# Expert stage of a decoder layer: another order of ScalarE and GpSimd work per block, and a down projection in three products of halves

## The chip, the core and the metric

The kernel runs on one core of a Trainium2 chip. The metric is device time in microseconds (us) of one execution. The core has a matrix engine (TensorE; PE in the rows, PEld its weight loads), VectorE (DVE), ScalarE (ACT), GpSimd (POOL), SyncE (SP), which here only issues transfers, and 16 DMA engines that all queues share. Each engine takes its own instructions in the order in which they are written. Engines wait for one another by semaphores.

## What is computed

One layer, depth 1, with 2048 tokens of width 1024: a gated linear recurrence with its projections, and then a mixture of 16 experts, two per token, and a last norm. The change lies in the expert stage:

```python
g = jnp.einsum('bsd,edf->bsef', h, w_gate)      # w_gate, w_up: 16 x 1024 x 256
u = jnp.einsum('bsd,edf->bsef', h, w_up)
act = jax.nn.silu(g) * u * gates[..., None]     # gates: two nonzero per token
out = jnp.einsum('bsef,efd->bsd', act, w_down)  # w_down: 16 x 256 x 1024
x = x + g2[:, None, :] * out
return rmsnorm(x, final_norm_g)
```

## The kernel before

Three stages follow one another: norm and recurrence (lines below 670), the output projection with routing (`out_and_route`), and the experts (`experts`, lines 1220 to 1668). Routing sorts the pairs of token and expert into **blocks** of 128 rows; each block belongs to one expert, and the 16 experts have 39 blocks together in this execution. The residual rows lie in DRAM as `x_slots` (`dr["x2"]`), by slot; the rows that the experts read lie in `hn_slots`.

A block `b` goes through these steps, each written as a small function:

- **TensorE** (`expert_tensor`): `turn` transposes the rows `e_xg` into PSUM (L1587). `gate_up` multiplies them with the gate and up weights, as three products of halves: high by high, high by low, low by high, 24 matmuls (L1610 to L1612). `turn_act` transposes the activation (L1618). `down` multiplies it with the down weights in fp32 (L1631), four matmuls of 512 columns, two records each in the trace. The loop runs `gate_up(i+2)` with `turn_act(i+1)` inside it, `turn(i+3)`, `down(i+1)`.
- **ScalarE** (`expert_scalar`): `tanh`, `high_x` (the high half of the rows, with `load_h`, which issues the load of the next `e_xg`), `high_a` (copies the turned activation to `e_ah`), `load_x` (issues the load of the residual rows `e_xa`), `square` (sum of squares of the new residual rows, L1454), `scale_row` (rows times the inverse root, to `e_obs`), `high_w` (high halves of the weights of an expert to come, in two parts of two quarters, each where it is due), and `index_acc` and `index_out` (the row numbers of the two scatters, L1432 and L1438).
- **VectorE** (`expert_vector`): `act_product`, `low_x`, `y_scaled` and `accumulate` (`e_ab` = down output plus `e_xa`, L1546), `low_w` (low halves of weights).
- **GpSimd** (`expert_gpsimd`): `scatter_acc` writes `e_ab` back to `x_slots` (L1316); `root` makes the inverse root in four small steps (L1340 to L1348); `weigh` multiplies `e_obs` with the norm's gain into `e_ob` (L1332); `scatter_out` scatters `e_ob` to the output (L1323).
- **SyncE** (`expert_sync`): 48 small loads of records (L1265), and the loads of the weights of 16 experts in four quarters each (`load_quarter`, L698 to L703). A quarter's buffer is loaded again once it is converted.

The order of the work is written out by hand. What matters below is which buffers exist once: `e_idx_o`, the row numbers of `scatter_out`, and `e_ob`, its rows. `index_out(b)` waits until `scatter_out(b-1)` has landed (`out_done`), `weigh(b)` too. `root(b)` waits for `square(b)`, `scale_row(b)` for `root(b)` and for `weigh(b-1)`, `square(b)` for `accumulate(b)`.

Of the kernel before, what the change touches and what calls it, by code (L numbers as in the profile page):

```python
# [4 lines left out]
F32 = mybir.dt.float32  # L5
# [677 lines left out]
QAT = (0, 3 * 2 * FE, 6 * 2 * FE, DOWN, WE)  # L683
QLOADS = (2, 2, 2, 1)
# [7 lines left out]
def load_quarter(sp, io, w, raws, i, q):  # L692


    raw, arrived = raws[q][:], w["in"][q]
    src = lambda t: io[t][0, expert_at(i)].rearrange("(k p) f -> p k f", p=P)
    if q == NQ - 1:
        sp.dma_start(raw.rearrange("p (k n) -> p k n", n=D), src("moe_w_down")).then_inc(arrived, 16)  # L698
    else:
        ks = slice(QAT[q] // (2 * FE), QAT[q + 1] // (2 * FE))  # L700
        dst = raw.rearrange("p (k a f) -> p k a f", a=2, f=FE)
        sp.dma_start(dst[:, :, 0], src("moe_w_gate")[:, ks]).then_inc(arrived, 16)
        sp.dma_start(dst[:, :, 1], src("moe_w_up")[:, ks]).then_inc(arrived, 16)  # L703


def out_and_route(nc, ctx, sem, cst, io, dr, tab, w, g2row):


    if True:
# [105 lines left out]
        def out_scalar(act):  # L815
# [26 lines left out]
            def high_w(q):  # L842
                act.wait_ge(w["in"][q], 16 * QLOADS[q])
                dst = w["hi"][:, QAT[q]:QAT[q + 1]] if q < NQ - 1 else w["dn"][:, 0:WE - DOWN]
                nc.scalar.activation(dst, w["raw"][q][:], ACT.Copy).then_inc(w["hi_done"], 1)
# [22 lines left out]
        def out_vector(dve):  # L868
# [123 lines left out]
            def low_w(q):  # L992

                dve.wait_ge(w["hi_done"], q + 1)
                wcols = slice(QAT[q], QAT[q + 1])
                v.tensor_tensor(w["lo"][:, wcols], w["raw"][q][:], w["hi"][:, wcols].bitcast(F32),
                                ALU.subtract).then_inc(w["lo_done"][q % 2], 1)
# [220 lines left out]
def experts(nc, ctx, sem, cst, io, tab, w, dr, g2row, out):  # L1218


    if True:
# [3 lines left out]
        raw1 = raw0[0:2] + [over(f"w_raw{q}_1", [P, QAT[q + 1] - QAT[q]], 0, F32, QAT[q] - QAT[2]) for q in (2, 3)]  # L1225
# [8 lines left out]
        ah = over("e_ah", [P, FE], 13)  # L1234
# [13 lines left out]
        av_turned, ah_ready = sem("av_turned"), sem("ah_ready")  # L1248
# [13 lines left out]
        def expert_sync(sp):  # L1262
# [17 lines left out]
            for e in range(2, E):  # L1280
                for q in range(NQ):
                    if q < NQ - 1:
                        sp.wait_ge(w["lo_done"][q % 2], (2 * e - 1, e, 2 * e)[q])
                    else:
                        sp.wait_ge(w["hi_done"], NQ * e)
# [6 lines left out]
        def convert_word(eng, b):  # L1292
# [3 lines left out]
            return ((v >> 1) & 1, v & 1), expert, (expert & 1) * DOWN, v >> 7  # L1296

        def low_w(dve, word):
            dues, e, off, before = word
            for part in range(2):  # L1300
                with dve.If(dues[part] == 1):
                    for q in ((0, 1), (2,))[part]:
                        dve.wait_ge(w["hi_done"], NQ * e + (q + 1))
                        dve.nop(nofuse=True)
                        cols = ds(off + QAT[q], QAT[q + 1] - QAT[q])
                        nc.vector.tensor_tensor(w["lo"][:, cols], raw1[q][:], w["hi"][:, cols].bitcast(F32),  # L1306
                                                ALU.subtract).then_inc(w["lo_done"][q % 2], 1)

        def expert_gpsimd(pool):
# [48 lines left out]
            for b in range(2):  # L1358
                weigh(b, b == 0)
                scatter_out(b)  # L1360
                scatter_acc(b + 1)
                root(b + 1)
# [14 lines left out]
        def expert_scalar(act):  # L1377
# [4 lines left out]
            def load_h(b):  # L1382
# [3 lines left out]
                row0 = slot_rows(act, b)  # L1386
# [4 lines left out]
            def load_x(b):  # L1391
# [3 lines left out]
                row0 = slot_rows(act, b)  # L1395
# [7 lines left out]
            def high_x(b, more=True):  # L1403
                if more:
                    load_h(b + 1)
# [9 lines left out]
            def high_w(b, first=False):  # L1415
                dues, e, off, before = convert_word(act, b)
                for part in range(2):
                    with act.If(dues[part] == 1):
                        if not first:
                            act.wait_ge(d_mm, before)  # L1420
                        for q in (2 * part, 2 * part + 1):
                            act.wait_ge(w["in"][q], (e + 1) * (16 * QLOADS[q]))
                            act.nop(nofuse=True)
                            dst = (w["hi"][:, ds(off + QAT[q], QAT[q + 1] - QAT[q])] if q < NQ - 1 else
                                   w["dn"][:, ds((e & 1) * (WE - DOWN), WE - DOWN)])
                            nc.scalar.activation(dst, raw1[q][:], ACT.Copy).then_inc(w["hi_done"], 1)  # L1426
# [29 lines left out]
            load_h(0)  # L1456
            act.wait_ge(w["sent_x"], 96)
            load_x(0)
            act.wait_ge(w["tabled"], 1)
            nless = blocks_less(act)  # L1460
            high_x(0)
            tanh(0)
            high_x(1)
            high_w(0, True)
            high_a(0)
            tanh(1)
            high_x(2)
# [3 lines left out]
            for b in range(LEAD):  # L1471
                square(b, b == 0)
                high_a(b + 1)
                load_x(b + 1)
                tanh(b + 2)
                high_x(b + 3)
                scale_row(b, b == 0)
                index_out(b, b == 0)
                high_w(b + 2)
                index_acc(b + 1)  # L1480
            act.wait_ge(rec_in[1], 16 * (MAXB - EARLY))
            with act.Fori(LEAD, nless) as i:
                square(i)
                high_a(i + 1)
                load_x(i + 1)
                tanh(i + 2)
                high_x(i + 3)
                scale_row(i)
                index_out(i)
                high_w(i + 2)  # L1490
                index_acc(i + 1)
            square(nless)
            high_a(nless + 1)
            load_x(nless + 1)
            tanh(nless + 2)
            scale_row(nless)
            index_out(nless)
            high_w(nless + 2)
            index_acc(nless + 1)
            square(nless + 1)  # L1500
            high_a(nless + 2)
            load_x(nless + 2)
# [8 lines left out]
        def expert_vector(dve):  # L1511
            def low_first(q):
                dve.wait_ge(w["hi_done"], q + 1)
                wcols = slice(QAT[q], QAT[q + 1])
# [19 lines left out]

            def y_scaled(b):
# [13 lines left out]
            low_first(2)  # L1549
            nless = blocks_less(dve)  # L1550
# [3 lines left out]
            dve.wait_ge(w["lo_done"][0], 2)  # L1554
            dve.wait_ge(w["hi_done"], NQ)
            low(0)
            act_product(1)
# [4 lines left out]
            for b in range(2):  # L1562
                act_product(b + 2)
# [192 lines left out]
```

## Time and profile before

| | us |
|---|---|
| median of 3 runs (1300.13 to 1301.42) | 1300.38 |
| the profiled execution | 1304.35 |
| its span, first to last instruction | 1302.7 |
| expert stage, from its first gate and up matmul to the end | 824.5 to 1302.7 |
| PE busy over the whole span | 1096.4 |
| DVE, ACT, POOL busy | 786.8, 631.4, 640.3 |

The times of instructions come from the profiled execution, on a clock that starts at its first instruction. An engine that is busy for half of the span can still set the time, where others wait for one of its instructions. In the rows a number in brackets is the idle time of the engine before the instruction, with the instruction or transfer that ended it; "issue" is no wait that the profile can name.

### The profile page before, as it was taken

The numbers are of one execution on the slowest core, as the hardware profiler recorded it, in microseconds if no ns is written. First come the engines' busy times: TensorE is split into PE (matmuls) and PEld (weight loads), VectorE is DVE, ScalarE is ACT, GpSimd is POOL, SyncE is SP. The second block draws the span as 40 slices with busy tenths as digits, with TensorE's granted clock in tenths as the row PEclk, the third lists the DMA queues.
The fourth block names the chain that finished last, engine by engine and source line by source line (L and its number), as shares of the span: only waits on it lengthen the run. The fifth ranks groups of instructions, "written<-read, shape, count | busy, mean of one in ns | idle before, by whom it ended". The sixth has DMA issues, their size and how long they took to land. (4 is left out here: it accounts for less than half of the span.)

```text
span 1302.7 us, 19169 instructions
## 1 busy us (share of the span) xinstructions
PE 1096.4 (84%) x4704; PEld 835.5 (64%) x4705; DVE 786.8 (60%) x1154; ACT 631.4 (48%) x928; POOL 640.3 (49%) x642
## 2 busy tenths in 40 slices
PE   1368999999999998389999981686989989999991
PEld 0256778787787786278888861564656666666660
DVE  6884667567667674535777767244555655556640
ACT  1464676676667566412222221234556656556641
POOL 0695626437246250022677667033646656565663
PEclk9999999999999999589999985697989999999995
DMA  8546244353344212661455537538668776778741
GB/s 303 179 99 202 82 134 117 116 161 105 109 133 149 97 56 90 213 225 66 162 178 204 201 121 273 177 112 290 231 243 284 273 270 232 255 261 280 257 137 65
DMA packets 143738, 232.60 MB, mean 179 GB/s; under 512 B 33728, under 2 KB 101312, under 8 KB 143056
## 3 DMA queue, kind: packets, MB, share of 16 engines
q1 hardware_dynamic: 108688, 128.20, 30.4%
q0 software_dynamic: 23632, 62.49, 13.4%
q10 hardware_dynamic: 11376, 41.42, 9.0%
q8 instruction: 17, 0.28, 0.1%
q14 instruction: 25, 0.20, 0.1%
HBM read 177.45 MB, written 91.31 MB: 206 GB/s over the span
## 5 line engine op out<-in xcount | busy, mean ns | idle before, releaser
L1631 PE MATMUL po<-w_dn,e_ah 128*128 (+1 forms) x312 | 147.8, 618 | 30.6 <-issue 20.4
L1610 PE MATMUL pl<-w_hi,e_xh 128*128 (+1 forms) x312 | 141.1, 452 | 15.7 <-DVE e_xl L1532 10.7
L1332 POOL TENSOR_TENSOR e_ob<-e_obs,e_fg 128x1024 f32<-128x1024 f32 x39 | 93.6, 2401 | 90.2 <-ACT e_idx_o L1438 77.0
L1165 PE MATMUL po<-wo_hi,b_yh 128*128 128x512 f32 x256 | 106.1, 414 | 27.6 <-DVE wo_lo L979 27.6
L1612 PE MATMUL pl<-w_hi,e_xl 128*128 (+1 forms) x312 | 125.2, 401 | 0.0
L1611 PE MATMUL pl<-w_lo,e_xh 128*128 (+1 forms) x312 | 124.6, 399 | 0.0
L1631 PEld LDWEIGHTS po<-w_dn,e_ah 128*128 128x128 f32 x312 | 58.5, 198 | 93.2 <-issue 92.9
L543 DVE SCALAR_TENSOR_TENSOR XB<-xu,conv_w,XB 128x512 f32<-128x512 f32 x96 | 91.6, 954 | 42.1 <-ACT XB L413 38.4
L636 PE MATMUL px<-hT_hi,wx_hi 128*128 128x512 f32 x256 | 101.8, 397 | 5.1 <-DVE wx_lo L477 5.1
L636 PE MATMUL pg<-hT_hi,wg_hi 128*128 128x512 f32 x256 | 104.2, 407 | 0.0
L1166 PE MATMUL po<-wo_lo,b_yh 128*128 128x512 f32 x256 | 102.3, 400 | 0.0
L1167 PE MATMUL po<-wo_hi,b_yl 128*128 128x512 f32 x256 | 102.3, 399 | 0.0
L637 PE MATMUL px<-hT_lo,wx_hi 128*128 128x512 f32 x256 | 101.5, 396 | 0.0
L638 PE MATMUL px<-hT_hi,wx_lo 128*128 128x512 f32 x256 | 101.4, 396 | 0.0
L638 PE MATMUL pg<-hT_hi,wg_lo 128*128 128x512 f32 x256 | 101.1, 395 | 0.0
L637 PE MATMUL pg<-hT_lo,wg_hi 128*128 128x512 f32 x256 | 101.1, 395 | 0.0
L612 POOL TENSOR_SCALAR macc<-stg,cond 128x512 f32<-128x512 f32 x8 | 11.5, 1437 | 153.9 <-PE pmod L659 149.3
L618 POOL TENSOR_TENSOR macc<-macc,mtmp 128x512 f32<-128x512 f32 x56 | 84.0, 1500 | 4.7
L1610 PEld LDWEIGHTS pl<-w_hi,e_xh 128*128 128x128 f32 x312 | 60.4, 194 | 38.7 <-issue 28.5
L1316 POOL DMA_INDIRECT x_slots<-e_ab,e_idx_a x38 | 44.9, 1181 | 78.6 <-DVE e_ab L1546 44.5
L1306 DVE TENSOR_TENSOR w_lo<-w_raw,w_hi 128x1536 f32 (+1 forms) x45 | 69.6, 1575 | 18.7 <-ACT w_hi L1426 18.3
L1546 DVE TENSOR_TENSOR e_ab<-po,e_xa 128x1024 f32<-128x1024 f32 x39 | 47.8, 1225 | 51.4 <-DMA x_slots<-e_ab,e_idx_a 31.4
(266 smaller groups left out, 2639.7 us busy)
## 6 DMA issues: line engine op xcount, KB each, us to landing
e_xg<-hn_slots ACTq DMA_DIRECT2D x40, 512.0 KB
e_xa<-x_slots ACTq DMA_DIRECT2D x39, 512.0 KB, 4.4
stg<-in_ada_w_dram POOLq DMA_DIRECT2D x32, 512.0 KB, 4.2
w_raw<-in_moe_w_down_dram SPq DMA_DIRECT2D x16, 1024.0 KB
w_raw<-in_moe_w_gate_dram SPq DMA_DIRECT2D x32, 384.0 KB
w_raw<-in_moe_w_up_dram SPq DMA_DIRECT2D x32, 384.0 KB
n_ada<-in_ada_w_dram SPq DMA_DIRECT2D x16, 512.0 KB, 4.9
n_x<-in_x_dram SPq DMA_DIRECT2D x16, 512.0 KB, 3.3
```

What stands on the lines that cost most here:

```text
L543: nc.vector.scalar_tensor_tensor(xb, xu[:, n, w:w + NB], cw[:, ds(j, 1), w], xb, ALU.mult, ALU.add).then_inc(done, 1)
L636: nc.tensor.matmul(dst[:], whi[br][:, k], hT_hi[:, k, cols], start=(k == 0), stop=False)
L637: nc.tensor.matmul(dst[:], whi[br][:, k], hT_lo[:, k, cols], start=False, stop=False)
L638: last = nc.tensor.matmul(dst[:], wlo[br][:, k], hT_hi[:, k, cols], start=False, stop=(k == KD - 1))
L1165: nc.tensor.matmul(po[u][:, hcols], yh[u][:, tok], wo_hi[:, k, hcols], start=(k == 0), stop=False)
L1166: nc.tensor.matmul(po[u][:, hcols], yh[u][:, tok], wo_lo[:, k, hcols], start=False, stop=False)
L1167: last = nc.tensor.matmul(po[u][:, hcols], yl[u][:, tok], wo_hi[:, k, hcols], start=False, stop=(k == KD - 1))
L1332: nc.gpsimd.tensor_tensor(ob[:], obs[:], fg[:], ALU.mult).then_inc(out_ready, 1)
L1610: nc.tensor.matmul(gu[:], xh[:, tok], hi, start=(k == 0), stop=False)
L1611: nc.tensor.matmul(gu[:], xh[:, tok], lo, start=False, stop=False)
L1612: last = nc.tensor.matmul(gu[:], xl[:, tok], hi, start=False, stop=(k == KD - 1))
L1631: last = nc.tensor.matmul(dst, ah[:, k * P:(k + 1) * P], rows, start=(k == 0), stop=(k == KF - 1))
```

## The change

There are three parts.

**The order of GpSimd and ScalarE.** A GpSimd iteration was `weigh(i)`, `scatter_out(i)`, `scatter_acc(i+1)`, `root(i+1)`; it is `scatter_acc(i+1)`, `root(i+1)`, `weigh(i)`, `scatter_out(i)`. On ScalarE `index_out(i)` goes from behind `scale_row(i)` to the end of the iteration, behind `high_w(i+2)` and `index_acc(i+1)`, and the two register loads of row numbers (`slot_rows`) go from `load_x` and `high_x` to the head of the iteration, ahead of `square(i)`. At the stage's start `high_x(0)`, `tanh(0)` and `high_x(1)` go ahead of the wait for the residual rows.

**The down projection.** The high half `e_ah` is now rounded to float32r, VectorE makes the low half `e_al` (`low_a`, at the head of its iteration), and `down` is three products of halves: 12 matmuls, waiting for `al_ready`. The down weights get high and low halves, as gate and up have.

**The quarters.** Each of the four quarters of an expert's weights now has 1536 columns (before: 1536, 1536, 1024 and 2048), with 2, 2, 3 and 2 transfers (before: 2, 2, 2 and 1). VectorE makes low halves of all four; before, of three. A quarter is loaded again when its low half is made.

```diff
-QAT = (0, 3 * 2 * FE, 6 * 2 * FE, DOWN, WE)
-QLOADS = (2, 2, 2, 1)
+QW = WE // NQ
+QLOADS = (2, 2, 3, 2)
...
-                    if q < NQ - 1:
-                        sp.wait_ge(w["lo_done"][q % 2], (2 * e - 1, e, 2 * e)[q])
-                    else:
-                        sp.wait_ge(w["hi_done"], NQ * e)
+                    sp.wait_ge(w["lo_done"][q % 2], 2 * e - 1 + q // 2)
...
             with pool.Fori(2, nless + 1) as i:
+                scatter_acc(i + 1)
+                root(i + 1)
                 weigh(i)
                 scatter_out(i)
-                scatter_acc(i + 1)
-                root(i + 1)
...
             with act.Fori(LEAD, nless) as i:
+                rows = slot_rows(act, i + 1), slot_rows(act, i + 4)
                 square(i)
                 high_a(i + 1)
-                load_x(i + 1)
+                load_x(i + 1, rows[0])
                 tanh(i + 2)
-                high_x(i + 3)
+                high_x(i + 3, rows[1])
                 scale_row(i)
-                index_out(i)
                 high_w(i + 2)
                 index_acc(i + 1)
+                index_out(i)
...
+            def low_a(b):
+                dve.wait_ge(ah_ready, b + 1)
+                nc.vector.tensor_tensor(al[:], pa[:, 0:FE], ah[:].bitcast(F32), ALU.subtract).then_inc(al_ready, 1)
...
             with dve.Fori(2, nless) as i:
+                low_a(i + 1)
                 act_product(i + 2)
...
-                pe.wait_ge(w["hi_done"], (e + 1) * NQ)
-                pe.wait_ge(ah_ready, b + 1)
+                pe.wait_ge(w["lo_done"][1], e * 2 + 2)
+                pe.wait_ge(al_ready, b + 1)
...
-                        rows = w["dn"][:, ds(off + (k * D + half * NB), NB)]
-                        last = nc.tensor.matmul(dst, ah[:, k * P:(k + 1) * P], rows, start=(k == 0), stop=(k == KF - 1))
+                        tok = slice(k * P, (k + 1) * P)
+                        hi, lo = [w[n][:, ds(off + (DOWN + k * D + half * NB), NB)] for n in ("hi", "lo")]
+                        nc.tensor.matmul(dst, ah[:, tok], hi, start=(k == 0), stop=False)
+                        nc.tensor.matmul(dst, ah[:, tok], lo, start=False, stop=False)
+                        last = nc.tensor.matmul(dst, al[:, tok], hi, start=False, stop=(k == KF - 1))
```

GpSimd, body of the block loop, before (`e_squared` is counted by `square`, `out_done` by the landed output scatter):

```order
L1331 REGISTER_ALU [waits scaled_row]
L1332 TENSOR_TENSOR e_ob<-e_obs,e_fg 128x1024 [waits out_done]
L1323 DMA out_dram<-e_ob,e_idx_o 2048x1024 [waits idx_o_ready,out_ready]
...
L1316 DMA x_slots<-e_ab,e_idx_a 32768x1024 [waits idx_a_ready,acc_ready]
L1340 TENSOR_TENSOR e_root<-e_ssq,b_nhalf 128x1 [waits e_squared,scaled_row]
...
L1348 TENSOR_TENSOR e_rstd<-e_root,e_part 128x1 [waits e_rstd_step]
```

The same loop after the change:

```order
L1319 DMA x_slots<-e_ab,e_idx_a 32768x1024 [waits idx_a_ready,acc_ready]
L1341 REGISTER_ALU [waits e_squared]
L1343 TENSOR_TENSOR e_root<-e_ssq,b_nhalf 128x1 [waits scaled_row]
...
L1351 TENSOR_TENSOR e_rstd<-e_root,e_part 128x1 [waits e_rstd_step]
L1334 REGISTER_ALU [waits scaled_row]
L1335 TENSOR_TENSOR e_ob<-e_obs,e_fg 128x1024 [waits out_done]
L1326 DMA out_dram<-e_ob,e_idx_o 2048x1024 [waits idx_o_ready,out_ready]
```

The multiplication into `e_ob` and the output scatter of block i now stand behind the root of block i+1 and its wait for `square(i+1)`.

ScalarE, end of one iteration of the block loop and head of the next, before:

```order
L1445 ACTIVATE e_obs<-e_ab,e_rstd 128x1024 [waits e_rstd,out_ready]
L1436 REGISTER_ALU
L1438 ISA [waits out_done]
L1438 ACTIVATE e_idx_o<-e_recs 128x1
...
L1432 ACTIVATE e_idx_a<-e_recs 128x1
L1482 ISA
L1482 COMPARE_AND_BRANCH
...
L1454 ACTIVATE e_sq,e_ssq<-e_ab 128x1025 [waits acc_ready,e_rstd]
```

The same place after the change (the rows behind the branch stand at the loop's head, and they run again in each turn):

```order
L1432 ACTIVATE e_idx_a<-e_recs 128x1
L1436 REGISTER_ALU
L1438 ISA [waits out_done]
L1438 ACTIVATE e_idx_o<-e_recs 128x1
L1485 ISA
L1485 COMPARE_AND_BRANCH
L1263 ISA
L1263 TENSOR_LOAD t_row
L1263 ISA x3
L1263 TENSOR_LOAD t_row
...
L1454 ACTIVATE e_sq,e_ssq<-e_ab 128x1025 [waits e_rstd]
```

The wait for the landed output scatter moved to the last place of the iteration, and two register loads stand between it and the next `square`.

## Rows read from the trace of the kernel before

**Rows 1.** Timeline (start us, us, engine, line): matmuls and weight loads of one product
```profile
904.37 0.19 PEld L1631 LDWEIGHTS po<-w_dn,e_ah 128*128 128x128 f32 x1 [0.24 <-issue]
904.80 0.19 PEld L1631 LDWEIGHTS po<-w_dn,e_ah 128*128 128x128 f32 x1 [0.24 <-issue]
...
907.63 0.39 PE L1612 MATMUL pl<-w_hi,e_xl 128*128 x1
...
907.86 0.40 PE L1610 MATMUL pl<-w_hi,e_xh 128*128 x1
```

**Rows 2.** Timeline, PE: the down projections of blocks 3, 20, 21 and 37
```profile
891.25 5.81 PE L1631 MATMUL po<-w_dn,e_ah 128*128 x8 [16.34 <-issue]
...
1088.40 3.60 PE L1631 MATMUL po<-w_dn,e_ah 128*128 x8
...
1098.44 1.88 PE L1631 MATMUL po<-w_dn,e_ah 128*128 x4
...
1264.23 3.70 PE L1631 MATMUL po<-w_dn,e_ah 128*128 x8 [0.72 <-issue]
```

**Rows 3.** Who waited for whom, expert stage (us in total, times, longest)
```profile
DVE e_ab L1546 <- DMA x_slots<-e_ab,e_idx_a: 31.4, 14, 5.2
...
ACT e_idx_o L1438 <- DMA out_dram<-e_ob,e_idx_o: 4.5, 3, 2.9
```

**Rows 4.** Timeline, ACT and POOL: square, root, weigh and output scatter
```profile
901.92 0.61 POOL L1340 TENSOR_TENSOR e_root<-e_ssq,b_nhalf 128x1 f32<-128x1 f32 x1
...
903.49 0.19 POOL L1348 TENSOR_TENSOR e_rstd<-e_root,e_part 128x1 f32<-128x1 f32 x1
...
907.78 2.40 POOL L1332 TENSOR_TENSOR e_ob<-e_obs,e_fg 128x1024 f32<-128x1024 f32 x1 [4.10 <-ACT e_idx_o L1438]
...
911.03 1.09 POOL L1323 DMA_INDIRECT out_dram<-e_ob,e_idx_o  x1 [0.85 <-issue]
...
1281.81 1.06 ACT L1454 ACTIVATE e_sq<-e_ab 128x1025 f32<-128x1025 f32 x1 [6.09 <-DVE e_ab L1546]
...
1283.14 0.57 POOL L1340 TENSOR_TENSOR e_root<-e_ssq,b_nhalf 128x1 f32<-128x1 f32 x1 [3.06 <-ACT e_sq L1454]
```

**Rows 5.** Timeline: an output scatter, and the index write that waited for it
```profile
1060.53 2.62 POOL L1323 DMA_INDIRECT out_dram<-e_ob,e_idx_o  x1 [2.01 <-DVE e_ab L1546]
...
1070.62 0.20 ACT L1438 ACTIVATE e_idx_o<-e_recs 128x1 int32 x1 [2.89 <-DMA out_dram<-e_ob,e_idx_o]
```

**Rows 6.** Line L1401, the 38 loads of `e_xa`, 512 KB each
```profile
DMA to landing us min/median/max: 3.2/4.5/8.6
```

**Rows 7.** Line L1257, register loads on ACT's sequencer (ns min/median/max)
```profile
L1257 ACTq FUSED_REGOPS  x144: 37/152/165, 822.1 to 1271.4; - x144
L1257 ACTq TENSOR_LOAD <-t_row x77: 273/286/1776, 821.8 to 1271.1; - x77
```

**Rows 8.** Timeline, blocks 37 and 38: square, high half, down; and a small VectorE step
```profile
903.35 0.42 DVE L1522 SCALAR_TENSOR_TENSOR e_th<-e_th,pl 128x256 f32<-128x256 f32 x1 [2.28 <-ACT e_th L1380]
...
1270.92 1.06 ACT L1454 ACTIVATE e_sq<-e_ab 128x1025 f32<-128x1025 f32 x1 [3.79 <-DVE e_ab L1546]
...
1271.98 0.36 ACT L1413 ACTIVATE e_ah<-prank 128x256 f32<-128x256 f32 x1
...
1272.64 6.26 PE L1631 MATMUL po<-w_dn,e_ah 128*128 x8 [4.49 <-ACT e_ah L1413]
```

**Rows 9.** Timeline: the third expert's weights, behind SyncE's record loads
```profile
879.14 0.43 SPq L702 DMA_DIRECT2D w_raw<-in_moe_w_gate_dram  x1
...
889.76 1.76 DVE L1306 TENSOR_TENSOR w_lo<-w_raw,w_hi 128x1536 f32 x1 [2.35 <-ACT w_hi L1426]
...
890.59 0.36 ACT L1413 ACTIVATE e_ah<-prank 128x256 f32<-128x256 f32 x1
```

**Rows 10.** Timeline, ACT: conversion for an expert of one block, both parts at once
```profile
950.10 3.80 ACT L1426 ACTIVATE w_hi<-w_raw 128x1536 f32 x3 [1.01 <-PE po L1631]
```

**Rows 11.** Timeline, POOL: the last output scatter; the span ends at 1302.7
```profile
1289.78 1.09 POOL L1323 DMA_INDIRECT out_dram<-e_ob,e_idx_o  x1 [0.86 <-issue]
```

More of the change, by code:

```diff
@@ L1224, in experts @@
         raw0 = w["raw"]
-        raw1 = raw0[0:2] + [over(f"w_raw{q}_1", [P, QAT[q + 1] - QAT[q]], 0, F32, QAT[q] - QAT[2]) for q in (2, 3)]
+        raw1 = raw0[0:2] + [over(f"w_raw{q}_1", [P, QW], 0, F32, (q - 2) * QW) for q in (2, 3)]
         xg = over("e_xg", [P, D], 3)
@@ L1233, in experts @@
         ab = ab_eps[:, 0:D]
-        ah = over("e_ah", [P, FE], 13)
+        ah, al = over("e_ah", [P, FE], 13, F32R), over("e_al", [P, FE], 13, F32R, FE)
         th, av = over("e_th", [P, FE], 13, F32, 2 * FE), over("e_av", [P, FE], 13, F32, 3 * FE)
@@ L1401, in load_x, with high_x @@
                 act.dma_start(xa[:], dr["x2"][ds(row0, P), :]).then_inc(xa_in, 16)
-            def high_x(b, more=True):
-                if more:
-                    load_h(b + 1)
+            def high_x(b, row0=None):
+                if row0 is not None:
+                    load_h(b + 1, row0)
                 act.wait_ge(turned, b + 1)
@@ L1553, in expert_vector @@
             low_x(1)
-            dve.wait_ge(w["lo_done"][0], 2)
-            dve.wait_ge(w["hi_done"], NQ)
+            for done in w["lo_done"]:
+                dve.wait_ge(done, 2)
             low(0)
+            low_a(0)
             act_product(1)
@@ L1562, in expert_vector @@
             for b in range(2):
+                low_a(b + 1)
                 act_product(b + 2)
@@ L1575, in expert_vector @@
                 low_w(dve, word)
+            low_a(nless + 1)
             act_product(nless + 2)
@@ L1579, in expert_vector @@
             low(nless + 2)
+            low_a(nless + 2)
             y_scaled(nless + 2)
@@ L1588, in turn, with expert_of @@
                 last.then_inc(turned, 1)
-            def expert_of(b, first, size):
+            def expert_of(b, first):
                 if first:
@@ L1593, in expert_of @@
                 e = per_block(pe, "expert", b, 0, E - 1)
-                return e, (e & 1) * size
+                return e, (e & 1) * WE
             def gate_up(b, first=False, turn_before=False):
-                e, off = expert_of(b, first, DOWN)
+                e, off = expert_of(b, first)
                 if not first:
@@ L1621, in down @@
             def down(b, first=False):
-                e, off = expert_of(b, first, WE - DOWN)
-                pe.wait_ge(w["hi_done"], (e + 1) * NQ)
-                pe.wait_ge(ah_ready, b + 1)
+                e, off = expert_of(b, first)
+                pe.wait_ge(w["lo_done"][1], e * 2 + 2)
+                pe.wait_ge(al_ready, b + 1)
                 if not first:
@@ L1691, in build @@
         tab["row0"] = sb("t_row0", [P, MAXB + 1], I32)
-        w = {"raw": [sb(f"w_raw{q}", [P, QAT[q + 1] - QAT[q]]) for q in range(2)], "in": [sem(f"raw_in{q}") for q in range(NQ)],
+        w = {"raw": [sb(f"w_raw{q}", [P, QW]) for q in range(2)], "in": [sem(f"raw_in{q}") for q in range(NQ)],
              "hi_done": sem("w_hi_done"), "lo_done": [sem("w_lo_done0"), sem("w_lo_done1")]}
@@ L1702, in build @@
             if n == "lo":
-                w["raw"] += [over(f"w_raw{q}_0", [P, QAT[q + 1] - QAT[q]], DOWN + QAT[q] - QAT[2], F32) for q in (2, 3)]
+                w["raw"] += [over(f"w_raw{q}_0", [P, QW], WE + (q - 2) * QW, F32) for q in (2, 3)]
             for i, name in enumerate(("gy", "hT") if n == "hi" else ("g1row", "sh2")):
```

88 lines of the change are left out of this document (47 added, 41 removed).

## The prediction

> **What bounds the kernel now.** I read the page first, then the timeline of each engine through the expert stage, then who waited for whom. Up to the expert stage the change touches nothing that costs time: the first four weight quarters are cut otherwise, with the same number of columns in all. So the sum is about the 39 blocks. Their clearest measure is the start of one down projection to the next. Where nothing is late this is 1098.44 - 1088.40 = 10.04 us, and the matrix engine is then never idle [rows 2]. The reader is to see in rows 2 that from block 3 to block 37 it takes 1264.23 - 891.25 = 372.98 us for 34 intervals, 10.97 on average. The other 0.93 us are waits, largest among them `accumulate` waiting until the scatter of the block before has landed, 31.4 us in 14 blocks [rows 3]. Blocks 0 to 2 run ahead of a wall: SyncE issues record loads until 879.1 and only then the third expert's weights [rows 9], so whatever the start of the stage gains ends there, and I cost the earlier `high_x(0)` at nothing. It would have to lose some 10 us before it showed, since the down projection before the stall ended well before that: the matrix engine sat idle for 16.34 us ahead of block 3 [rows 2].
>
> **The down projection** itself gets cheaper. An fp32 record takes 904.80 - 904.37 = 0.43 us and there are 8 per block, 3.44 us. A product of halves starts 907.86 - 907.63 = 0.23 us after the one before [rows 1], and 12 are 2.76 us. The matrix engine's own block becomes 10.04 - 0.68 = 9.36 us. Against that, `down` now waits for `low_a` as well. No row shows it; the nearest is a VectorE step on as many columns from PSUM, 0.42 us [rows 8], so with the handover some 0.55 us. Its bounds are nothing (hidden behind `turn`) and 1 us. The low half of the down weights is 2048 columns more per expert on VectorE: 1.76 us for 1536 columns [rows 9], so 2.3 us per expert, or about 1 per block, on an engine that is far from full; I cost it at nothing as long as VectorE waits elsewhere.
>
> **The new order** is what I think decides. Follow one turn of the four steps that now hang together. `square(b)` lets `root(b)` start 1283.14 - 1281.81 = 1.33 us after its own start; `root` takes 903.49 + 0.19 - 901.92 = 1.76; `weigh(b-1)`, which now stands behind it, starts about 0.1 later, and from its start to the issue of `scatter_out(b-1)` there are 911.03 - 907.78 = 3.25 [rows 4]. That is 6.44 us. Then the scatter has to land, because `index_out(b)` waits for it, and `index_out(b)` is now the last thing ScalarE does ahead of `square(b+1)`. So the ring is closed: one block can't be shorter than 6.44 us, the landing, and what ScalarE needs from the landing to the next `square`. The last is a wake-up and the branch (about 0.4) and two register loads that now stand in between, each 0.29 + 0.15 plus gaps [rows 7], about 0.6; with the start of `square` I take 1.7 us (bounds 1.2, and 3 if the loads take their slower form of up to 1.8 us). In the kernel before there was no such ring: `scatter_out(b-1)` was issued without waiting for `square(b)`, so it had landed when `index_out(b)` came, which waited 3 times only [rows 3].
>
> **The landing** is the term that I can't read directly. The wait that did occur gives the upper end: issued at 1060.53, index written at 1070.62, 10.1 us, with the weights of the next expert in flight [rows 5]. The lower end is the nearest transfer of equal size, the load of `e_xa`: 3.2 us at the least, 4.5 at the median, 8.6 at most [rows 6]. The output scatter is issued 6.4 us after `square(b)`, when `e_xa` (issued after `high_a`) and the previous residual scatter should be done and the next one isn't issued, so it should do better than the median; but weights are in flight in most blocks. I take 4.0, nearest to the median of rows 6, less a little for the quiet place. A block is then 6.44 + 4.0 + 1.7 = 12.15 us.
>
> Nothing else in the block is longer. From `square(b)` the high half comes 1.06 later and `down` 0.66 after that [rows 8]; with `low_a` it starts about 2.3 after `square(b)`, takes 3, and VectorE's two steps follow, so `accumulate(b+1)` is done some 8 us after `square(b)`, well within 12. `scale_row(b)` waits for `weigh(b-1)`, 5.5 us after `square(b)`, and a part of `high_w` (3 us) ends before 10. The matrix engine has 2.8 us of slack per block; its saved 0.68 us falls into that slack and is worth nothing.
>
> **The sum**, against the profiled execution of 1304.35 us:
> - To the down projection of block 3: two more transfers in expert 1's load push the record loads and the wall by 1.0 us (0.5 each), and `low_a` has to follow `low_w`, which ended at 889.76 + 1.76 = 891.52 where `down` had its input at 890.59 + 0.36 [rows 9]: with `index_out` ahead of `square`, 0.8. Together +1.8.
> - 34 intervals: 34 x 12.15 = 413.1, less 372.98: +40.1.
> - The expert with one block, whose conversion is done in one go (three pieces in 3.80 us and one more) [rows 10]: VectorE has four low quarters, 4 x 1.76 = 7.0 us, in a row, about 2 us more than the ring hides: +2.0.
> - The tail. `square(37)` came 1270.92 - 1264.23 = 6.7 us after `down(37)`; in the ring it comes 12.15 - 2.35 = 9.8 after: +3.1. From there to the last scatter there were 1289.78 - 1270.92 = 18.9 us [rows 2, 8, 11]; now `weigh(37)` waits for the landing of `scatter_out(36)` (6.44 + about 3.5), and it, its scatter, `root(38)`, `scale_row(38)` and `weigh(38)` follow, 20.6 in all: +1.7. Together +4.8.
>
> 1304.35 + 1.8 + 40.1 + 2.0 + 4.8 = 1353.05. The profiled execution was 1304.35 - 1300.38 = 3.97 above the median of the runs; taking that off gives **1349 us**, 3.7% slower.
>
> **Rivals.**
> 1. *The ring with a quick landing*, 3.2 us, the least of rows 6, since by then the other transfers are done. The block is 11.34 us, 34 x 0.81 = 27.5 less: 1322 us. For it speaks the place of the issue, against it that every expert brings weights. The Trainium skill ("DMA: Bandwidth & Descriptors", section "Anatomy of one DMA — SWDGE (gpsimd) path") gives a DMA of this path 2.0 us plus its bytes over 436 GB/s, and says the completion receipt from HBM makes most of the fixed part; by that 512 KB would take an estimated 3.2 us and the time would be that of this rival. The waits of rows 5 are three times as long, so the trace agrees with it for an idle chip at best.
> 2. *The ring with a slow landing*, 5.5 us, because the shifted scatter now meets the weights that before started behind it: 34 x 1.5 = 51 more, 1400 us. Rows 5 speak for it.
> 3. *Faster: the ring doesn't bind*, and the matrix engine's saving shows. `scatter_acc` goes ahead of `weigh`, so the waits of rows 3 don't grow, and a block is 10.97 - 0.68 = 10.29 us: 34 x 0.68 = 23.1 less, with +1.8 at the start and +1.7 in the tail: 1304.35 - 23.1 + 3.5 - 3.97 = 1281 us. It takes a landing below 10.29 - 8.14 = 2.15 us; the break-even against before lies near a landing of 2.6, and no transfer of this size in rows 6 took less than 3.2.
>
> **How the numbers follow.** Landing between 3.5 and 4.8, my forecast: 1332 to 1376, 0.50. Rival 1 (down to 3.0, 1315 to 1332): 0.18. Rival 2 (1376 to 1417): 0.17. Rival 3: 0.10. The rest, 0.05, lies between rival 3 and 1315, 0.03 of it within 0.2% of before, which is about what a measurement of this kernel can tell from no change. The range 1316 to 1395 holds the forecast, rival 1 and the better part of rival 2, 0.8. Faster 0.10, same 0.03, slower 0.87.
>
> **What would show it.** In the profile after: `e_idx_o` waits on the DMA of `out_dram` in nearly all blocks, 1 to 4 us each; down projections start about 12 us apart (matmul pitch 0.23); the matrix engine idles 2 to 3 us ahead of each, put down to `e_ah`, `e_al` or "issue"; `accumulate` hardly waits for the residual scatter. The forecast is wrong in its size if the landings are other than 4 us, and in kind if `e_idx_o` hardly waits, or if `down` is held by VectorE's `low_w` instead.

## Result, and the profile after

The changed kernel takes 1351.89 us (median of 4 runs, 1346.08 to 1354.61), the kernel before 1300.45 in the same session: a ratio of 1.0388, 95% interval 1.0349 to 1.0428. The forecast of 1349 us and its sign held. The profiled execution took 1354.61 us, its span is 1353.0.

| | before | after |
|---|---|---|
| span, us | 1302.7 | 1353.0 |
| down projection of block 3 starts | 891.25 | 895.15 |
| 34 intervals to block 37 | 372.98 | 415.27 |
| one interval | 10.97 | 12.21 |
| from block 37 to the end of the span | 38.5 | 42.6 |

The down projections answer to [rows 2]. Timeline of after, PE: first matmuls of blocks 3, 14, 15 and 37. Start us, us, engine and line, then in brackets the idle time before:

```profile
895.15 0.79 PE L1647 MATMUL po<-w_hi,e_ah 128*128 x1 [23.13 <-DVE w_lo L1308]
...
1034.60 0.49 PE L1647 MATMUL po<-w_hi,e_ah 128*128 x1 [0.86 <-issue]
...
1046.74 0.49 PE L1647 MATMUL po<-w_hi,e_ah 128*128 x1 [0.98 <-issue]
...
1310.42 0.49 PE L1647 MATMUL po<-w_hi,e_ah 128*128 x1 [1.19 <-issue]
```

Blocks 14 and 15 stand 12.14 us apart, a typical pair. The busy time of the engines says little about it. First section of the page of after:

```profile
PE 1093.0 (81%) x4860; PEld 880.9 (65%) x4861; DVE 841.7 (62%) x1209; ACT 632.7 (47%) x928; POOL 630.2 (47%) x642
```

No engine is over 81% busy, and the kernel is slower all the same. What sets the time is a ring of steps, and a turn of it can be read off the timeline. ACT and POOL of after, from the `square` of one block to the next:

```profile
1032.37 1.06 ACT L1454 ACTIVATE e_sq<-e_ab 128x1025 f32<-128x1025 f32 x1 [1.37 <-issue]
...
1033.75 0.57 POOL L1343 TENSOR_TENSOR e_root<-e_ssq,b_nhalf 128x1 f32<-128x1 f32 x1 [1.19 <-ACT e_sq L1454]
...
1035.43 2.39 POOL L1335 TENSOR_TENSOR e_ob<-e_obs,e_fg 128x1024 f32<-128x1024 f32 x1
...
1038.66 1.09 POOL L1326 DMA_INDIRECT out_dram<-e_ob,e_idx_o  x1 [0.85 <-issue]
...
1042.97 0.20 ACT L1438 ACTIVATE e_idx_o<-e_recs 128x1 int32 x1 [0.57 <-DMA out_dram<-e_ob,e_idx_o]
...
1044.55 1.06 ACT L1454 ACTIVATE e_sq<-e_ab 128x1025 f32<-128x1025 f32 x1 [1.37 <-issue]
```

From `square` to the issue of the scatter there are 1038.66 - 1032.37 = 6.29 us, then 4.31 until the index is written, and 1.58 until the next `square`: 12.18. Who waited for whom in after, from 825 us to the end (us in total, times, longest), for [rows 3]:

```profile
POOL x_slots L1319 <- ACT e_idx_a L1432: 112.9, 25, 26.8
ACT e_obs L1445 <- POOL e_ob L1335: 89.4, 32, 4.2
...
ACT e_idx_o L1438 <- DMA out_dram<-e_ob,e_idx_o: 41.3, 26, 3.8
...
ACT e_sq L1454 <- issue: 39.3, 29, 1.5
...
PE po L1647 <- DVE w_lo L1308: 24.8, 2, 23.1
...
DVE e_ab L1555 <- DMA x_slots<-e_ab,e_idx_a: 16.4, 9, 4.4
```

`e_idx_o` waited for the landing 3 times, 4.5 us in all, before; now 26 times, 41.3 us, 1.6 on average. In the eight of the 33 turns between blocks 4 and 37 in which it doesn't wait, the landing takes 2.2 to 3.4 us. `accumulate`, whose 31.4 us were the largest wait before, is down to 16.4. The two rows at the top are not in the ring that I forecast. They belong to a second one, below.

### The profile page after: what moved, and what is told of

Same layout as the page of the kernel before. It is cut to its first block and busy times, and to the rows that moved or that the text cites. A ratio compares the mean times of both kernels' runs of the same rounds, so it can differ in the third digit from the quotient of the medians.

```text
span 1353.0 us, 19727 instructions
## 1 busy us (share of the span) xinstructions
PE 1093.0 (81%) x4860; PEld 880.9 (65%) x4861; DVE 841.7 (62%) x1209; ACT 632.7 (47%) x928; POOL 630.2 (47%) x642
## 5 line engine op out<-in xcount | busy, mean ns | idle before, releaser
L1319 POOL DMA_INDIRECT x_slots<-e_ab,e_idx_a x38 | 62.5, 1644 | 179.7 <-ACT e_idx_a L1432 112.9
L1647 PE MATMUL po<-w_hi,e_ah 128*128 (+1 forms) x156 | 74.1, 475 | 83.3 <-issue 47.4
L1625 PE MATMUL pl<-w_hi,e_xh 128*128 (+1 forms) x312 | 129.1, 414 | 9.4 <-DVE w_lo L1308 4.9
L1308 DVE TENSOR_TENSOR w_lo<-w_raw,w_hi 128x1536 f32 x60 | 102.7, 1753 | 31.3 <-ACT w_hi L1425 30.8
L1425 ACT ACTIVATE w_hi<-w_raw 128x1536 f32 x60 | 86.0, 1480 | 35.1 <-DMA w_raw<-in_moe_w_up_dram 23.6
L1647 PEld LDWEIGHTS po<-w_hi,e_ah 128*128 128x128 f32 x156 | 34.2, 219 | 97.6 <-issue 91.2
L1445 ACT ACTIVATE e_obs<-e_ab,e_rstd 128x1024 f32<-128x1024 f32 x39 | 45.0, 1153 | 97.1 <-POOL e_ob L1335 89.4
L1546 DVE TENSOR_TENSOR po<-po,g2row 128x1024 f32<-128x1024 f32 x39 | 48.1, 1233 | 63.5 <-PE po L1649 63.5
```

The source lines that it names most:

```text
L1308: nc.vector.tensor_tensor(w["lo"][:, ds(off + q * QW, QW)], raw1[q][:], w["hi"][:, ds(off + q * QW, QW)].bitcast(F32), ALU.subtract).then_ ...
L1625: nc.tensor.matmul(gu[:], xh[:, tok], hi, start=(k == 0), stop=False)
L1647: nc.tensor.matmul(dst, ah[:, tok], hi, start=(k == 0), stop=False)
```

## Experiments

All were timed in three rounds beside the kernel before. "Block" is the mean interval from the down projection of block 3 to that of block 37. Each diff is against the changed kernel unless it says otherwise.

### The two halves of the change

**order_only** is the kernel before with the new order of GpSimd and ScalarE; the down projection stays fp32 and the quarters stay as they were. Diff against before:

```diff
             with pool.Fori(2, nless + 1) as i:
+                scatter_acc(i + 1)
+                root(i + 1)
                 weigh(i)
                 scatter_out(i)
-                scatter_acc(i + 1)
-                root(i + 1)
...
                 scale_row(i)
-                index_out(i)
                 high_w(i + 2)
                 index_acc(i + 1)
+                index_out(i)
```

> The kernel before with the new order of GpSimd and ScalarE work alone; the down projection stays in fp32 and the weight quarters stay as before. Ring theory (square(b), root(b), weigh(b-1), scatter_out(b-1) landed, index_out(b), two register loads, square(b+1)): the ring doesn't contain the matrix engine, so the time is that of the full change, 1348 us (1338 to 1356). Rival theory (the loss comes from the down projection: low_a, more low halves on VectorE, more transfers): 1290 to 1310 us.

Measured: 1349.00 us, ratio 1.0353 (1.0309 to 1.0398), block 12.25. The order alone gives nearly the whole loss.

**down_only** is the other half: products of halves and new quarters, with the loops of both engines in the old order.

```diff
             with pool.Fori(2, nless + 1) as i:
+                weigh(i)
+                scatter_out(i)
                 scatter_acc(i + 1)
                 root(i + 1)
-                weigh(i)
-                scatter_out(i)
...
                 scale_row(i)
+                index_out(i)
                 high_w(i + 2)
                 index_acc(i + 1)
-                index_out(i)
```

> The full change with the block loops of GpSimd and ScalarE, and the places of the register loads in them, as they were before; down projection in three products of halves and the new quarters stay. Ring theory: the ring is open, the matrix engine's saving of 0.68 us per block shows, about 1283 us (1274 to 1292). Rival theory (the down projection costs): 1330 us or more.

Measured: 1314.25 us, 1.0072 (1.0009 to 1.0135), block 11.41. A miss by 31 us, with the other sign: without the new order the products of halves and the new quarters cost about 9 us by the ratio (1 to 18 by its interval), 12 by the medians. Who waited for whom between 900 and 1250 us, down_only:

```profile
PE po L1650 <- DVE w_lo L1308: 17.7, 9, 3.1
PE prank L1636 <- DVE w_lo L1308: 17.3, 5, 4.0
```

and in the same stretch of the kernel before:

```profile
PE prank L1618 <- DVE w_lo L1306: 6.8, 6, 2.1
```

TensorE waits for VectorE behind its low halves of weights. What that does is seen in one place of down_only's timeline (DVE and PE):

```profile
1006.80 1.23 DVE L1558 TENSOR_TENSOR e_ab<-po,e_xa 128x1024 f32<-128x1024 f32 x1 [3.09 <-DMA x_slots<-e_ab,e_idx_a]
...
1007.94 3.42 DVE L1308 TENSOR_TENSOR w_lo<-w_raw,w_hi 128x1536 f32 x2
1009.74 0.69 PE L1636 MATMUL prank<-ident,e_av 128*128 128x128 f32 x2 [3.23 <-DVE w_lo L1308]
...
1011.08 0.63 PE L1630 MATMUL pl<-w_hi,e_xl 128*128 x1
...
1011.51 0.63 PE L1628 MATMUL pl<-w_hi,e_xh 128*128 x1
```

`accumulate` waited 3.09 us for the residual scatter, the two low halves stand behind it, TensorE waited 3.23 us, and after that its matmuls start 0.43 us apart where [rows 1] show 0.23; the granted clock from 1009 to 1015 us is 0.50.

### Which move makes the ring

**pool_old** puts only GpSimd's loop back, ScalarE keeps the new order.

```diff
             with pool.Fori(2, nless + 1) as i:
+                weigh(i)
+                scatter_out(i)
                 scatter_acc(i + 1)
                 root(i + 1)
-                weigh(i)
-                scatter_out(i)
```

> The full change with GpSimd's loop alone in its order from before (weigh(i), scatter_out(i), scatter_acc(i+1), root(i+1)); ScalarE keeps index_out last and the register loads at the head. Ring theory: scatter_out(b-1) no longer waits for square(b), so it has landed long before index_out(b); the longest remaining path through scale_row, high_w, the loads, square and root is about 9.4 us, and the time is near 1283 us (1272 to 1296). Rival theory (the place of index_out and of the register loads on ScalarE is the cause by itself): 1335 us or more.

Measured: 1342.21 us, 1.0312 (1.0256 to 1.0368), block 12.08. A miss. The forecast ring is opened, and another closes. pool_old, 860 to 1320 us:

```profile
POOL e_ob L1335 <- DMA out_dram<-e_ob,e_idx_o: 66.4, 23, 5.1
...
DVE e_ab L1555 <- DMA x_slots<-e_ab,e_idx_a: 58.8, 27, 4.9
...
POOL out_dram L1326 <- ACT e_idx_o L1438: 51.8, 11, 26.1
```

The late index holds `scatter_out(b)`, its landing holds `weigh(b+1)`, and `scatter_acc` stands behind that, so `accumulate` waits for a landing.

**idx_back** puts only `index_out` back behind `scale_row`; GpSimd keeps the new order.

```diff
                 scale_row(i)
+                index_out(i)
                 high_w(i + 2)
                 index_acc(i + 1)
-                index_out(i)
```

> The full change with index_out alone back behind scale_row, ahead of high_w and index_acc; GpSimd keeps its new order. Ring theory: the wait for the landed output scatter stays in the ring, and high_w (3.3 us in some 28 of 34 blocks) now stands behind it instead of beside it, so a block takes about 15 us and the time is about 1430 us (1400 to 1460). Rival theory (moving index_out to the end was the mistake): back to 1300 us or less.

Measured: 1470.43 us, 1.1296 (1.1248 to 1.1345), block 15.67. The direction is as expected, the time 10 us above the range. So with GpSimd's new order the move of `index_out` saves 118 us; the loss would be three times as large without it. Timeline of idx_back, ACT and POOL, the longer ring:

```profile
1007.51 1.09 POOL L1326 DMA_INDIRECT out_dram<-e_ob,e_idx_o  x1 [0.85 <-issue]
1010.85 0.20 ACT L1438 ACTIVATE e_idx_o<-e_recs 128x1 int32 x1 [2.95 <-DMA out_dram<-e_ob,e_idx_o]
1012.39 2.86 ACT L1425 ACTIVATE w_hi<-w_raw 128x1536 f32 x2 [1.34 <-issue]
1015.15 0.19 ACT L1432 ACTIVATE e_idx_a<-e_recs 128x1 int32 x1
...
1016.21 2.25 POOL L1319 DMA_INDIRECT x_slots<-e_ab,e_idx_a  x1 [7.60 <-ACT e_idx_a L1432]
```

The weights' high halves (2.86 us) now lie behind the landing, and the residual scatter, with its row numbers at 1015.15, behind them: GpSimd idles 7.60 us.

**loads_back** takes the two register loads out of the ring.

```diff
             with act.Fori(LEAD, nless) as i:
-                rows = slot_rows(act, i + 1), slot_rows(act, i + 4)
...
             def load_x(b, row0=None):
...
+                row0 = slot_rows(act, b)
```

> The full change with the register loads of row numbers in the block loop back in load_x and high_x, everything else as changed. Ring theory: the loads stand in the ring between index_out(b) and square(b+1), where 1.58 us go by in the changed kernel; without them about 0.35, so each of some 29 blocks gets 1.2 us shorter: 1352 - 35 = 1317 us (1308 to 1328). If the wait for the landed scatter isn't in the ring, or another path is equally long: 1340 to 1352.

Measured: 1335.14 us, 1.0249 (1.0217 to 1.028), block 11.67, against 1317 expected and above the range: half of the gain came. The step from the index to `square` fell as expected. loads_back, the end of a turn, and one `root`:

```profile
1023.28 0.20 ACT L1441 ACTIVATE e_idx_o<-e_recs 128x1 int32 x1 [0.45 <-DMA out_dram<-e_ob,e_idx_o]
1023.70 1.06 ACT L1457 ACTIVATE e_sq<-e_ab 128x1025 f32<-128x1025 f32 x1 [0.21 <-issue]
...
1023.70 1.68 POOL L1319 DMA_INDIRECT x_slots<-e_ab,e_idx_a  x1 [3.26 <-DVE e_ab L1558]
1025.38 1.25 POOL L1343 TENSOR_TENSOR e_root<-e_ssq,b_nhalf 128x1 f32<-128x1 f32 x1
...
1030.99 1.09 POOL L1326 DMA_INDIRECT out_dram<-e_ob,e_idx_o  x1 [0.85 <-issue]
```

It is 0.42 us now instead of 1.58. But `root` starts behind `scatter_acc`, which GpSimd begins only at the same moment as `square`, and from `square` to the issue of the scatter it takes 7.29 us here (mean of blocks 4 to 36: 6.92, in after 6.46). The loads were partly cover for it.

### Opening the rings

**pool_idx** lets GpSimd write the output's row numbers itself, so that ScalarE waits for no landing.

```diff
             def scatter_out(b):
+                nc.gpsimd.tensor_copy(idx_o[:], recs[:, ds(b, 1), 1]).then_inc(idx_o_ready, 1)
                 pool.wait_ge(idx_o_ready, b + 1)
...
             def index_out(b, first=False):
+                return
```

> The full change, but GpSimd writes e_idx_o itself right ahead of scatter_out, so ScalarE never waits for the landed output scatter. This opens the ring through the landing and leaves a second one: scale_row(b), high_w (2.9 us where due), the register loads, square(b+1), root(b+1), weigh(b), scale_row(b+1), which adds up to 11.6 to 11.9 us in blocks with a part of high_w and 9 in others. Theory: 1332 us (1322 to 1342), a gain over the full change of 10 to 30 us. If the landing was the only bound: 1300 or less; if it was none: 1352.

Measured: 1325.72 us, 1.0190 (1.016 to 1.022), block 11.43, in the range. **pool_idx_loads** has both edits, this one and that of loads_back.

> Both edits: GpSimd writes e_idx_o, and the register loads are back in load_x and high_x. The ring through the landing is gone and the second one is some 1.2 us shorter (10.4 in blocks with a part of high_w), so GpSimd's new order should cost little by itself: 1308 us (1298 to 1320), near the 1314 of the kernel with the old order. If GpSimd's new order costs for another reason (the residual scatter, VectorE): 1325 or more.

Measured: 1325.00 us, 1.0183 (1.0153 to 1.0213), block 11.49: no change from pool_idx, and a miss by 17 us. With the landing out of ScalarE's way the loads are worth nothing, and what holds the block at 11.4 to 11.5 is the second ring. One turn in pool_idx_loads:

```profile
1026.53 1.15 ACT L1452 ACTIVATE e_obs<-e_ab,e_rstd 128x1024 f32<-128x1024 f32 x1 [3.00 <-POOL e_ob L1336]
1028.07 2.86 ACT L1431 ACTIVATE w_hi<-w_raw 128x1536 f32 x2 [0.38 <-issue]
1030.83 0.19 ACT L1438 ACTIVATE e_idx_a<-e_recs 128x1 int32 x1
...
1031.88 2.25 POOL L1319 DMA_INDIRECT x_slots<-e_ab,e_idx_a  x1 [3.33 <-ACT e_idx_a L1438]
1034.14 0.60 POOL L1344 TENSOR_TENSOR e_root<-e_ssq,b_nhalf 128x1 f32<-128x1 f32 x1
...
1035.84 2.40 POOL L1336 TENSOR_TENSOR e_ob<-e_obs,e_fg 128x1024 f32<-128x1024 f32 x1
...
1038.33 1.15 ACT L1452 ACTIVATE e_obs<-e_ab,e_rstd 128x1024 f32<-128x1024 f32 x1 [2.27 <-POOL e_ob L1336]
```

`scale_row` waits for `weigh`, which stands behind `root`, behind `scatter_acc`, which waits for `index_acc`, which stands behind `high_w` and `scale_row`: 1038.33 - 1026.53 = 11.8 us. No transfer has to land in this turn. Between 900 and 1250 us `scatter_acc` is held by `e_idx_a` 19 times (66.9 us) and by `accumulate` 10 times (31.4 us), so the ring closes in many blocks, not in all.

**pool_both_loads** takes `index_acc` out of that ring too. The diff is against pool_idx_loads:

```diff
             def scatter_acc(b):
+                if not (isinstance(b, int) and b == 0):
+                    pool.wait_ge(acc_out, b * 16)
+                pool.nop(nofuse=True)
+                nc.gpsimd.tensor_copy(idx_a[:], recs[:, ds(b, 1), 0]).then_inc(idx_a_ready, 1)
                 pool.wait_ge(idx_a_ready, b + 1)
...
             def index_acc(b, first=False):
+                return
```

> GpSimd writes both e_idx_o and e_idx_a itself, register loads back in load_x and high_x, the rest as in the full change. With e_idx_o alone on GpSimd the block stood at 11.4 us, with or without the register loads. Theory: the ring that was left goes through the other index: scale_row(b), high_w, index_acc(b+1), scatter_acc(b+1), root(b+1), weigh(b), scale_row(b+1): 1.15 + 0.4 + 2.87 + 0.2 + 0.85 + 1.5 + 1.76 + 0.1 + 2.4 + 0.1 = 11.3 us. With e_idx_a on GpSimd the longest is 10.3 to 10.6: 1298 us (1288 to 1308). If that ring isn't it (landing of the residual scatter, VectorE): 1318 or more.

Measured: 1298.14 us, 0.9972 (0.9938 to 1.0007), block 10.77, in the range. So the whole loss by the order is gone once neither index comes from ScalarE (the register loads, which pool_idx_loads shows to be worth nothing here, are in `load_x` and `high_x` again). It is level with the kernel before, not ahead of it. But it is 16 us below down_only, which has the same products of halves and the old order, and the two intervals of the ratio just don't overlap. Whether that is GpSimd's order or its index writes isn't shown: the old order with both indices on GpSimd was not run.

### Why the products of halves cost time

**cut_old** is down_only with the old cut of the quarters. Diff against down_only, its first lines:

```diff
-QW = WE // NQ
-QLOADS = (2, 2, 3, 2)
+QAT = (0, 3 * 2 * FE, 6 * 2 * FE, DOWN, WE)
+QLOADS = (2, 2, 2, 1)
```

> The order of before, the down projection in three products of halves, but the weight quarters cut as before (1536, 1536, 1024, 2048 columns), with a low half of the last quarter too. In the kernel with the new cut (1314 us) gate_up waited at its seventh step for the low half of the third quarter, up to 3.6 us, and the TensorE clock fell behind the wait. Theory: the third quarter is ready (1.48 - 1.06) + (1.76 - 1.22) = 0.96 us earlier, the longest waits stay under the 3 us at which the clock fell, and some 14 of these blocks save 1 to 2 us each: 1296 us (1286 to 1304). Rival (VectorE's extra low halves as such cost, low_a queued behind low_w): 1310 to 1316.

Measured: 1312.00 us, 1.0089 (1.0062 to 1.0117), a miss by 16 us. Between 900 and 1250 us the waits at `turn_act` for a low half fell from the 17.3 us of down_only to 3.9, and `down` still waits 14.3 us for one, up to 3.3 at a time (17.7 in down_only). The time hardly changed, so the cut isn't it; the rival of that run held. The profiled execution was the fastest of the four (1304.38), with a block of 11.17.

**four_products** adds the product of both low halves to down_only, 16 matmuls of halves per block for 12.

```diff
                         nc.tensor.matmul(dst, ah[:, tok], lo, start=False, stop=False)
+                        nc.tensor.matmul(dst, al[:, tok], lo, start=False, stop=False)
```

> The order of before with the down projection in products of halves (1314 us), and the fourth product, low by low, added: 16 matmuls per block in place of 12, 3.7 us of TensorE in place of 2.8, more than fp32's 3.44. Clock theory (with 12 products TensorE reaches its wait for the third quarter's low half sooner, waits longer, and its clock falls to half behind it): the added 0.9 us fills the wait and the clock stays up, 1300 to 1308 us. VectorE theory (low_a and the down weights' low halves delay accumulate and the next quarter): no gain from it, 1314 to 1330 us.

Measured: 1314.26 us, 1.0108 (1.0043 to 1.0173), block 11.23. The stretch from 900 to 1250 us (us, then busy us and instructions of PE, PEld, DVE, ACT, POOL; granted clock; DMA share; GB/s), of the kernel before:

```profile
900.00:1250.00 350.00, 329.23 (x1343) 226.40 (x1342) 205.90 (x232) 208.13 (x340) 205.47 (x223) 0.99 0.74 255
```

The same of down_only:

```profile
900.00:1250.00 350.00, 307.06 (x1400) 248.07 (x1398) 234.12 (x263) 199.35 (x324) 207.08 (x211) 0.94 0.71 246
```

The same of four_products:

```profile
900.00:1250.00 350.00, 330.76 (x1559) 269.52 (x1559) 241.84 (x271) 203.31 (x334) 208.56 (x218) 0.98 0.71 250
```

With more work the clock is back at 0.98 from 0.94, and the time is the same. TensorE is busy 23.7 us longer in this stretch, and the waits of `down` and `turn_act` for low halves fell from 35.0 us to 8.8: the added work fills waits. That speaks against the lower clock and against TensorE's own work (0.9 us per block more) as what sets the block of down_only. That the two just offset each other, the run by itself doesn't exclude. VectorE has 234 us busy for 206 before.

**two_products** is cut_old without the product with the down weights' low half and without that half on VectorE; the waits on it go too, and the last quarter is loaded again when its high half is made, as in the kernel before. Diff against cut_old:

```diff
                 with dve.If(dues[part] == 1):
-                    for q in (2 * part, 2 * part + 1):
+                    for q in ((0, 1), (2,))[part]:
...
                         nc.tensor.matmul(dst, ah[:, tok], hi, start=(k == 0), stop=False)
-                        nc.tensor.matmul(dst, ah[:, tok], lo, start=False, stop=False)
                         last = nc.tensor.matmul(dst, al[:, tok], hi, start=False, stop=(k == KF - 1))
```

> The order of before, old cut of the quarters, down as two products, high by high and low by high: the product with the down weights' low half is left out, and VectorE doesn't make that half. low_a stays. TensorE's down is 8 matmuls, 1.8 us. VectorE theory (its 2.3 us per expert of added low halves are the cost of the new down): below 1300 us, about 1292. Clock theory (idle TensorE loses its clock, and the block is bound by the landing of the residual scatter anyway): 1305 to 1318 us.

Measured: 1291.27 us, 0.9916 (0.9875 to 0.9957), block 10.75. That is 21 us below cut_old. Of the matmuls' waits on low halves of weights between 900 and 1250 us this is left:

```profile
PE pl L1624 <- DVE w_lo L1305: 5.9, 1, 5.9
...
PE prank L1632 <- DVE w_lo L1305: 3.0, 2, 2.6
```

That is 8.9 us for 23.1 in cut_old. The 34 intervals got 14.0 us shorter between the two profiled executions (379.65 and 365.65), so the waits that went are as large as what the blocks gained. If TensorE's work is free here, as four_products suggests, the 21 us come from VectorE's extra half, from the waits on it, or from the earlier load of the last quarter. This run takes away all three and doesn't tell them apart.

### Is GpSimd's new order worth anything by itself?

**free_fp32** is the kernel before with GpSimd's new order, both indices written by GpSimd, and `e_obs` in two buffers, so that `scale_row` doesn't wait for `weigh` of the block before. Diff against before:

```diff
-        obs = over("e_obs", [P, D], 14)
+        obs2 = over("e_obs", [P, 2 * D], 14)
...
-                if not first:
-                    act.wait_ge(out_ready, b)
+                if not (first or isinstance(b, int) and b < 2):
+                    act.wait_ge(out_ready, b - 1)
```

> The kernel before (fp32 down, old quarters, register loads where they were) with GpSimd's new order, both indices written by GpSimd, and e_obs twice, so that scale_row(b) waits for weigh(b-2) only. No ring through weigh, index writes or landings of the output scatter is left; what stays is the matrix engine's 10.04 us per block and the landing of the residual scatter, issued at once behind accumulate: 10.3 us per block, 34 x 0.6 = 20 us less than before: 1280 us (1268 to 1292). If GpSimd's new order costs by itself: 1300 or more.

Measured: 1298.96 us, 0.9987 (0.9957 to 1.0017), block 10.74; a miss by 19 us. A block got 0.23 us shorter, not 0.6. The same stretch as above:

```profile
900.00:1250.00 350.00, 335.90 (x1373) 230.55 (x1372) 208.49 (x237) 204.98 (x283) 219.37 (x296) 0.99 0.74 258
```

TensorE is busy 335.9 of 350 us. With fp32 there is little left to gain, and the new order gains nothing that can be measured.

With products of halves and the new quarters, the four orders together:

| order of GpSimd | order of ScalarE | kernel | us |
|---|---|---|---|
| old | old | down_only | 1314 |
| old | new | pool_old | 1342 |
| new | new | after | 1352 |
| new | old, but for the loads | idx_back | 1470 |

## Why the prediction was right, point by point

- **The ring.** Right, in its steps and its sizes. Over blocks 4 to 36 of after: from `square` to the issue of the scatter 6.46 us on average (forecast 6.44), to its landing 3.90 (4.0; it ranges from 2.2 to 5.6), from there to the next `square` 1.79, median 1.75 (1.7). A turn is 12.15, as forecast. The 4.0 was a choice between rows that reach from 3.2 to 8.6, and a hit within 0.1 us is luck as much as reading. order_only shows that it is the order. pool_idx shows that 26 of the 51 us go through ScalarE's wait for the landing; the rest goes with the second ring (pool_both_loads).
- **34 intervals**, with the 2.0 us for the expert of one block: forecast +42.1, measured 415.27 - 372.98 = +42.3. The interval into the one-block expert took 15.98 us, 3.9 more than the mean of the others, where I had said 2 more. The others average 12.10, so two small errors offset each other.
- **The first term** was mis-sized: +1.8 forecast, 895.15 - 891.25 = +3.9 measured, and not for the reasons that I gave. The lateness is there ahead of the blocks, at SyncE's first record load: before, then after, with the load that ends the wall:

```profile
821.42 4.81 SPq L1265 DMA_DIRECT2D e_recs<-rec_scratch  x5
```
```profile
826.16 4.79 SPq L1271 DMA_DIRECT2D e_recs<-rec_scratch  x5
...
883.70 0.43 SPq L702 DMA_DIRECT2D w_raw<-in_moe_w_gate_dram  x1
```

  The first record load comes 4.7 us later in after, the wall 4.6 (879.14 before), block 3 3.9. From the first record load on, block 3 is 0.8 us earlier, where I had put +1.0 for the transfers and +0.8 for `low_a`. Over all the kernels here the first record load lies between 816.4 and 826.2 us, block 3 between 884.7 and 895.2, and the distance of the two only between 67.5 and 71.8. So most of the +3.9 is how long the earlier stages took in these two executions; kernels with the new quarters and with the old ones overlap there (818.4 to 826.2 and 816.4 to 823.5). The gain of the early `high_x(0)` did end at the wall: counted from the first record load, block 0 is 6.3 us earlier in after.
- **The tail**: +4.8 forecast; 42.6 - 38.5 = +4.1 measured.
- **The signs** came in weaker than written. `e_idx_o` waited for the landing 26 times of 39, 1.6 us on average, where I had said nearly all blocks and 1 to 4 us. TensorE idles 1.7 us on average ahead of a down projection (28 times under "issue", 47.4 us), against 2 to 3 forecast. `accumulate` still waits 16.4 us for the residual scatter, about half of before.
- **Rival 1**, the quick landing of 3.2 us, fell: the mean is 3.90. By the Trainium skill ("DMA: Bandwidth & Descriptors", section "Anatomy of one DMA — SWDGE (gpsimd) path") the estimate was 3.2; the trace of after is 0.7 above it. **Rival 2**, 5.5 us, is the upper end of single landings, not their mean.
- **Where the prediction would have failed without the ring.** I wrote that the low half of the down weights costs nothing "as long as VectorE waits elsewhere", and rival 3 priced a kernel without the ring at 1281 us. down_only has no such ring and takes 1314. VectorE's half stands ahead of work that TensorE waits for, and two_products puts up to 21 us on it. Nor is it a fixed price: pool_both_loads has VectorE's half too and takes 1298. In after it is hidden behind the ring: order_only, without it, takes 1349 and after 1352.
- **What I didn't see**: the ring has company. `scale_row`, `high_w`, `index_acc`, `scatter_acc`, `root`, `weigh` form a second one. With it the block is 11.4 us, only 0.8 shorter. Opening the first (pool_idx) therefore gives 26 us only, and the block stays at 11.43, where rival 3 had put a kernel without a ring at 10.29.

## What to carry to other kernels

Before moving a step, follow the waits from it round to itself across the engines, with every single-buffered tile and every landing in the loop; the sum of that ring is the shortest possible block, however idle the engines are. Look for the next longest ring too, since it caps what the mend is worth. A step that an idle engine can take for free by its busy share still costs time if it stands ahead of something that the bounding engine waits for.

## What the runs showed of the hardware

- The output scatters of 512 KB landed 2.2 to 5.6 us after their issue, 3.9 on average, in the same loop. Ahead of nearly every GpSimd row of such a scatter GpSimd is idle for 0.83 to 0.86 us (from block 3 on, 35 of 36 in before and 36 of 36 in after), for 0.87 to 0.91 where it writes the index itself (pool_idx).
- Two register loads at the head of ScalarE's loop cost 1.16 us, about the 0.6 each that the prediction has: the step from the index to `square` is 1.58 us with them and 0.42 without (after, loads_back). The load's own row is half of that. After, register loads (ns min/median/max), for [rows 7]:

```profile
L1263 ACTq TENSOR_LOAD <-t_row x77: 272/278/533, 818.0 to 1307.5; - x77
```

- The slowest load takes 533 ns in after, where [rows 7] show 1776. The other kernels with the loads at the head have 864 to 1099 (order_only, pool_old, idx_back, pool_idx), loads_back has 1118. Why is not shown.
- TensorE's granted clock differs with how it is fed: 0.94 in the stretch of down_only, 0.98 with a third more matmuls per down projection, at the same time of the kernel. In down_only's timeline above, matmuls behind a wait of 3.23 us start 0.43 us apart, at a granted clock of 0.50, the lower of the two levels.

What stays open: how two_products' 21 us divide between VectorE's time, the waits on the low half and the earlier load of the last quarter, and why the stages ahead of the experts end up to 10 us apart from one profiled execution to another. No variant with the full computation is measurably faster than the kernel before.
